# First weights of an output projection loaded and split inside the scan of the delta rule

## The reference, cut to what matters

```python
def step(S, inp):                      # one chunk of the gated delta rule, per head
    q_c, k_c, u_c, w_c, g_c, a_c = inp
    v_new = u_c - jnp.einsum('bhcd,bhde->bhce', w_c, S)
    o = jnp.einsum('bhcd,bhde->bhce', q_c * jnp.exp(g_c)[..., None], S) + jnp.einsum('bhcs,bhse->bhce', a_c, v_new)
    ...
o_f = _gated_delta_chunked(dq, dk, dv, g_f, beta_f)
o_b = flip(_gated_delta_chunked(flip(dq), flip(dk), flip(dv), flip(g_b), flip(beta_b)))
o = (o_f + o_b).transpose(0, 2, 1, 3)
o = o * lax.rsqrt(jnp.mean(o * o, axis=-1, keepdims=True) + EPS) * dn_norm_w
o = o * jax.nn.silu(heads(dz, DN_HEADS))
delta = o.reshape(B, L, DN_WIDTH)
y = jnp.einsum('ble,ed->bld', jnp.concatenate([attn, delta], axis=-1), w_out)
return x + y
```

## Time and profile before

| | |
|---|---|
| time before, median of 3 runs | 2832.3 us (2832.14 to 2832.37) |
| the profiled execution's own time | 2832.62 us |
| its span in the trace | 2830.8 us |
| PE busy | 2679.3 us, 95% of the span |
| DVE, ACT, POOL busy | 1174.1, 1072.3 and 1243.0 us |
| mean granted clock of TensorE | 0.977 of full speed |

### The profile page before, as it was taken

One profiled execution on the slowest core, in us unless ns is written; L12 is line 12 of the kernel. 1 busy time (PEld: TensorE's weight loads), 2 busy tenths in 40 slices (PEclk: granted clock), 3 DMA queues, 4 the chain that ended last, 5 costly groups with the idle time before them and its releaser, 6 DMA issues.

```text
span 2830.8 us, 33041 instructions
## 1 busy us (share of the span) xinstructions
PE 2679.3 (95%) x13337; PEld 2150.5 (76%) x13337; DVE 1174.1 (41%) x1631; ACT 1072.3 (38%) x1593; POOL 1243.0 (44%) x717
## 2 busy tenths in 40 slices
PE   6999998988969999999999999899999999999997
PEld 4778875667858888887888777666788888788885
DVE  6465666655663222222222327667532222222223
ACT  4443445634544422233322333656443222232222
POOL 2222222554026555556555554311455454565554
PEclk8999998989989999999999999999999999999998
DMA  3222415441143222223222232100222222323331
GB/s 132 90 88 96 150 45 203 135 142 52 38 145 115 97 97 97 97 97 104 97 97 97 98 130 91 40 8 1 99 95 98 97 97 97 112 90 108 116 103 69
DMA packets 93880, 273.20 MB, mean 97 GB/s; under 512 B 25944, under 2 KB 26136, under 8 KB 93600
## 3 DMA queue, kind: packets, MB, share of 16 engines
q1 hardware_dynamic: 93728, 271.09, 28.2%
HBM read 240.05 MB, written 31.00 MB: 96 GB/s over the span
## 4 chain that ended last, share of the span: by engine, by line
PE 82%; DVE 6%; POOL 5%; ACT 3%; DMA 2%; issue 1%; SPq 1%; POOLq 0%; DVEq 0%; ACTq 0%
PE ps L350 23%; PE ps L351 23%; PE ps L352 23%; PE ps L875 2%; ACT t L366 2%; PE ps L895 2%; PE ps L859 2%; POOL t L1336 1%; POOL t L1333 1%; PE ps L491 1%; DVE t L1009 1%; PE ps L1437 1%; POOL t L1834 1%; POOL t L415 1%; ACT t L958 1%
## 5 line engine op out<-in xcount | busy, mean ns | idle before, releaser
L366 ACT ACTIVATE t<-t 128x1024 fp32r<-128x1024 f32 (+5 forms) x961 | 735.3, 810 | 1392.1 <-PE ps L352 650.6
L415 POOL TENSOR_TENSOR t<-t 128x1024 fp32r<-128x1024 f32 x356 | 862.5, 2427 | 874.7 <-ACT t L366 874.6
L350 PE MATMUL ps<-t 128*128 128x512 f32 (+1 forms) x3034 | 1199.0, 395 | 47.5 <-DVE t L528 18.4
L352 PE MATMUL ps<-t 128*128 128x512 f32 (+1 forms) x3034 | 1181.4, 389 | 0.0
L351 PE MATMUL ps<-t 128*128 128x512 f32 (+1 forms) x3034 | 1181.3, 389 | 0.0
L350 PEld LDWEIGHTS ps<-t 128*128 128x128 f32 x3034 | 572.0, 189 | 184.8 <-issue 53.0
L351 PEld LDWEIGHTS ps<-t 128*128 128x128 f32 x3034 | 572.5, 189 | 120.7 <-issue 6.5
L352 PEld LDWEIGHTS ps<-t 128*128 128x128 f32 x3034 | 571.9, 188 | 118.5
L2050 DVE SCALAR_TENSOR_TENSOR t<-ps,t 128x512 f32<-128x512 f32 x192 | 132.7, 691 | 315.0 <-PE ps L352 277.2
L2106 POOL TENSOR_TENSOR t<-t 128x512 fp32r<-128x512 f32 x84 | 108.7, 1295 | 332.4 <-ACT t L366 332.4
L2027 DVE TENSOR_TENSOR t<-ps,t 128x512 f32<-128x512 f32 x84 | 58.1, 692 | 396.2 <-PE ps L352 396.2
(11 more groups left out here) (167 smaller groups left out, 1884.6 us busy)
## 6 DMA issues: line engine op xcount, KB each, us to landing
t<-in_wts_dram SPq DMA_DIRECT2D x356, 512.0 KB, 3.5
t<-pj SPq DMA_DIRECT2D x39, 512.0 KB, 5.9
pj<-t SPq DMA_DIRECT2D x32, 512.0 KB, 2.7
t<-in_rpb_dram SPq DMA_DIRECT2D x8, 736.0 KB, 7.7
t<-in_xT_dram SPq DMA_DIRECT2D x8, 512.0 KB, 10.5
t<-grow_d SPq DMA_DIRECT2D x8, 512.0 KB, 8.4
t<-beta_d SPq DMA_DIRECT2D x8, 512.0 KB, 9.5
t<-in_xT_dram SPq DMA_DIRECT2D x16, 256.0 KB, 4.0
```

Of the source, the lines that this page charges most:

```text
L350: e.matmul(out, ah, bh, start=start, stop=False)
L352: return e.matmul(out, al, bh, start=False, stop=stop)
L366: return e.activation(out, in_, fn, scale=scale)
L415: e.tensor_tensor(lo[:], T.raw[n % NR][:], hi[:].bitcast(F), SUB).then_inc(*w_lo.up(n))
```

## The change

The weight buffers move to the right side of SBUF, over what heads 0 and 1 of the delta rule leave. For that the right side is stacked in another order, with `D_.Y` and `D_.R` innermost, so that the four `raw` places and the first two `sp` places lie over `dm`, `D_.D`, `D_.k` and the part of `D_.Y` that is no longer read. SP issues the loads of tiles 33 to 36 in the delta rule's stage, behind a wait for `o_var` of head 1. ACT rounds tiles 33 and 34 in the second scan, in the hooks 9 and 11 (the second halves of steps 4 and 5). POOL subtracts for both in `pool_delta`. The three places in the output projection's code that did this are removed. The work itself stays the same: no instruction is added or removed.

```diff
-    def weight_buffers(st):
-        return [sb(st, [128, 1024]) for _ in range(NR)], [(sb(st, [128, 1024], R), sb(st, [128, 1024], R))
-                                                         for _ in range(NS)]
+    def weight_buffers(st, side=None):
+        return ([sb(st, [128, 1024], side=side) for _ in range(NR)],
+                [(sb(st, [128, 1024], R, side=side), sb(st, [128, 1024], R, side=side)) for _ in range(NS)])
...
     D_.dm = sb(early, [128, 4, 128], side="right")
-    D_.R, D_.Y, D_.D = ([[sb(early, [128, L], side="right") for _ in range(2)] for _ in range(2)] for _ in range(3))
+    D_.D = [[sb(early, [128, L], side="right") for _ in range(2)] for _ in range(2)]
     D_.k = [sb(early, [128, L], side="right") for _ in range(2)]
+    D_.Y, D_.R = ([[sb(early, [128, L], side="right") for _ in range(2)] for _ in range(2)] for _ in range(2))
...
-    B_.raw, B_.sp = weight_buffers(bb)
+    B_.raw, B_.sp = weight_buffers(bb, "right")
...
     def act_delta(e, w):
...
-        scan(1, banks_1, lambda i: [finish(h, part) for h, part in ends_of.get(i, [])])
+
+        def ends(i):
+            for h, part in ends_of.get(i, []):
+                finish(h, part)
+            if i in (9, 11):
+                act_weights(e, w, N_INPROJ + (i - 9) // 2)
+        scan(1, banks_1, ends)
...
     def pool_delta(e, w):
...
         for _ in blocks(e, w, 1):
             pass
+        for n in range(2):
+            pool_weights(e, w, N_INPROJ + n)
...
     def sp_delta(e, w):
...
         z(0)
         z(1)
+        w.wait_ge(o_var, 1)
+        for n in range(N_INPROJ, N_INPROJ + NR):
+            sp_weights(e, w, n)
         w.wait_ge(s_po, (0, 1, 7))
...
     def act_outproj(e, w, P):
...
         for i, k in enumerate(P.order):
-            if P is OUT1 and i == 1:
-                act_weights(e, w, P.first)
             large(0, k)
-        if P is OUT1:
-            act_weights(e, w, P.first + 1)
...
     def pool_outproj(e, w, P):
-        if P is OUT1:
-            pool_weights(e, w, P.first)
-            pool_weights(e, w, P.first + 1)
...
     def sp_all(e, w):
...
-        for n in range(N_INPROJ, N_INPROJ + NR):
-            sp_weights(e, w, n)
```

## The result

The change makes the kernel slower. The median of 7 runs is 2841.82 us (2840.98 to 2845.76), beside 2832.37 us (2831.75 to 2836.51) for 7 runs of the kernel before. The ratio is 1.0031 with a 95% interval of 1.0019 to 1.0043. The forecast was 2824.1 us, in a range that ended at 2828.8.

The account below looks back on a forecast made before the run. PE was taken to bound the kernel, with two waits behind the barrier before its solid run. The terms -8.2 + 0 + 0 from the 2832.3 us median gave 2824.1 us, with an 8-in-10 range of 2822.3 to 2828.8.

Parts of the forecast that it names:

- The start of the projection: Behind the barrier: with tiles 33 and 34 ready, PE starts at DVE's first `Lo`; tile 34 begins 8.2 us earlier.
- rival C: Delta-rule scan: POOL's stops of DVE open PE gaps, the clock falls in steps 5 to 7; 2842.7 us, chance 0.04.
- rival B: Projection start: the clock stays low through tile 33, groups take 1.35 us each; 2828.0 us, chance 0.10.
- ACT in the scan: Scan steps 4 and 5: two roundings of 1.06 us fit ACT's idle gaps; cost 0 to 0.1 us, taken as 0.
- POOL in the scan: Scan steps 4 and 5: two subtractions of 2.35 us don't disturb DVE; cost 0, other end 4.7 us.
- rival A: Delta-rule scan: each of POOL's two subtractions stops DVE for up to 2.35 us; 2828.8 us, chance 0.10.
- The loads and the parked parts: Tile loads land six us before ACT needs them, and X parts are there in time; cost 0.
- Behind it: After tile 34 begins: tile 35 is ready in time, PE stays without gaps, and the whole gain lasts.

Follow-up runs that it names:

- right_192: The changed kernel with a 192-byte pad ahead of the weight buffers on the right, so weights start at 32 modulo 256 like the data: 2824.78 us, ratio 0.9968.
- layout_192: The kernel before with all weight buffers on the right and a 192-byte pad, loads and splits left where they were: 2832.05 us, ratio 0.9995.
- layout_only: The kernel before with all later-stage weight buffers moved to the right, without a pad, loads and splits left where they were: 2848.87 us, ratio 1.0055.
- two_right: The changed kernel, but only tiles 33 and 34 have buffers on the right; later tiles use the left as before: 2826.39 us, ratio 0.9975.
- the sweeps: Separate kernels running only the three-matmul pattern on constant data, with weights and data at varied SBUF places: 680.0 to 703.1 ns a group.
- right_64: The changed kernel with a 64-byte pad ahead of the weight buffers on the right, so all ten lie 64 bytes lower: 2864.17 us, ratio 1.0110.
- left_64w: The kernel before with the six rounded weight buffers 64 bytes higher on the left: 2849.35 us, ratio 1.0052.

## Why the prediction was wrong

By its own steps:

- **The start of the projection, -8.2 us.** Right in its mechanism, and a little large. From DVE's last end ahead of the barrier, at 817.35, to tile 34, at 826.74, it is 9.4 us now, and it was 834.92 - 818.15 = 16.8: 7.4 us won. The first `Lo` released PE, and no group waited. The clock took one group more to rise: three groups at about 1.3 us (819.08 to 823.06) where I had taken two, as before. `right_192` needed four. So part of rival B is real. That tile 34 began at 826.74, as forecast, is luck: tile 33 took 7.66 us and not 6.88, and the scan ended 0.8 us early for a reason that the forecast didn't have (rival C below). What the early splits are worth by themselves is measured: 7.3 us is what `right_192` (2824.78) has over `layout_192` (2832.05), with the same layout on the same chip.
- **ACT in the scan, 0.** Right. ACT's timeline of the changed kernel, in steps 4 and 5:

```profile
786.28 1.05 ACT L367 ACTIVATE t<-t 128x1024 fp32r<-128x1024 f32 x1
787.45 1.71 ACT L367 ACTIVATE t<-ps,t 128x128 f32<-128x128 f32 x4
...
791.34 1.05 ACT L367 ACTIVATE t<-t 128x1024 fp32r<-128x1024 f32 x1
792.50 1.71 ACT L367 ACTIVATE t<-ps,t 128x128 f32<-128x128 f32 x4
```

The roundings fill the gaps of the earlier trace rows, and the output copies stay 5.05 us apart.

- **POOL in the scan (rival A), 0.** Right. POOL subtracts at 787.41 and 792.46, and DVE's three scan lines in this time read as before (ns min/median/max):

```profile
L1572 DVE SCALAR_TENSOR_TENSOR t<-ps,t x10: 342/342/345, 789.5 to 799.8; 128x128 f32<-128x128 f32 x10
L1582 DVE SCALAR_TENSOR_TENSOR t<-t,ps x12: 337/343/349, 786.3 to 797.2; 128x128 f32<-128x128 f32 x12
L1593 DVE TENSOR_TENSOR t<-t,ps x12: 282/289/289, 787.9 to 799.4; 128x128 f32<-128x128 f32 x12
```

The Trainium skill (SBUF — State Buffer, section "SBUF: two separate sides") says that only DVE instructions with two SBUF inputs or in a two-port mode need the ports shared with GpSimd; this trace agrees, with 349 ns as the longest.

- **The loads and the parked parts, 0.** Right. The four loads were issued from 774.22, landed within 7.5 us, and nobody waited for them.
- **Rival C, the slower one.** It did not happen. The granted clock was at 0.50 twice in the second scan of the kernel before:

```profile
756.90:763.73 6.83, 5.02 (x24) 4.76 (x24) 2.34 (x9) 3.73 (x12) 0.00 (x0) 0.50 0.49 189
784.21:787.62 3.41, 3.41 (x19) 3.41 (x18) 0.93 (x3) 1.11 (x4) 0.00 (x0) 0.50 0.00 0
```

In the changed kernel it was at 0.50 in step 0 again (758.59 to 765.42), and from there to the end of the scan at full speed:

```profile
765.42:806.38 40.96, 33.51 (x280) 31.88 (x279) 31.29 (x90) 21.33 (x66) 4.72 (x2) 1.00 0.22 78
```

So the low stretch of step 4 is missing, and the scan ended 0.8 us earlier. The change is not what removed it: `right_192`, with the same order of work, has it (0.50 from 783.62 to 787.03). The prediction said that only a state such as step 4's speaks for C, and that it lasted less than a step; the one in step 0, 6.83 us long, it left out. C's 2842.7 us lies 0.9 from the measured time by chance, since no part of its mechanism took place.
- **The step that failed is "Behind it":** "PE had no gap from 835.00 to 1200.00 with the same order of work, so I expect the whole gain to last." The order of work was the same and the gaps stayed away, but the time of one matmul did not stay the same. I priced every instruction that the change moves, and gave the move of the buffers themselves no term at all. It costs 6.6 ns for each of 2506 groups, 16.5 us, twice what the early splits bring. `layout_only` shows it alone (14.5 us over its medians), and `right_192` shows it gone.

The term was not to be had from the trace before, in which all groups have distance 0 modulo 256 and run at 680 ns. The diff shows the move, though, and a cost of unknown size for 2506 groups on the path that bounds the kernel should have widened the range at the slower side.

`right_192` and `two_right` beat both kernels, at 8.3 and 8.0 us under the kernel before.

## What to carry to other kernels

Where TensorE bounds a kernel, moving its operands in SBUF is an edit with a price of its own, even if no instruction changes. After such an edit, count matmuls in a stretch where PE is busy throughout and compare with before: the busy share, the clock and the recorded durations all stay the same while the pace changes by 1 to 3%. For matmuls of this form (128x512, split into high and low parts), let weights and data start at the same place modulo 256 bytes; a pad of 192 bytes was worth 17 to 18 us here (the ratio to the kernel before is 1.0031 without it and 0.9968 with it). When a gain ahead of a long solid run doesn't arrive, subtract the start of the run from the end of the span in both traces before looking for a wait.

## What the runs showed of the hardware

The pace of these matmuls depends on the distance of weights and data in SBUF modulo 256 bytes: 680 ns for three at 0, 686 to 687 at 192, and 697 to 703 at the other multiples of 32. Neither the absolute place, nor the distance in large, nor which end of SBUF they lie at changed it, and it is the same with the rest of the chip at rest. The means near 687 and 700 lie one and three steps of 6.67 ns above 680; those near 697 and 703 lie on no such step.

What stays open is why the distance counts, and why +64 costs 20 ns and -64 only 7. Open too are the first ten tiles of the output projection in the changed kernel, which ran at 700.0 ns and fell to 687 at a single float32 matmul, at the distance where `layout_only` and the sweeps had 686 to 687 from the start; they are worth 76 x 13.3 ns = 1.0 us. `right_64` does the same, with 700.0 ns in its first ten tiles and 697 from the same float32 matmul on. Both have the early splits and no wait in tile 33. `layout_only` and `left_64w`, which have the old start, don't show it, and neither does `right_192`, which has the new start at distance 0. So at other distances the way a run of PE begins seems to count a little too, but no run was made to show it.
